# A fused decoder layer: the first transfers from one small tensor, through one queue, and 34 warm-up products instead of 40

## What is computed

```python
h = rms_norm(x, norm_w[l], NORM_EPS)          # x: 256 x 2048
proj = h @ w_in[l]                            # all float32
o_a = nsa_mixer(...)                          # its compression uses cmp_k_w1, cmp_v_w1 (4096 x 512 each)
o_b = diff_mixer(...)
mixed = jnp.concatenate([o_a * jax.nn.silu(z_a), o_b * jax.nn.silu(z_b)], axis=-1)
x = x + mixed @ w_out[l]
return rms_norm(x, final_norm_w, NORM_EPS)
```

## Time and profile before

| | |
|---|---|
| median of 3 runs | 494.6 us (493.87 to 495.35) |
| profiled execution, its time | 495.11 us |
| its span in the trace | 493.3 us |
| TensorE busy | 482.1 us (98%) |
| chain that ended last, share of TensorE | 96% |
| HBM read | 105.20 MB |

### The profile page before, as it was taken

How to read it: one execution, slowest core, us unless ns; L and a number is a source line. 1 busy time by engine, 2 the same in 40 slices (tenths; PEclk the granted TensorE clock), 3 DMA queues, 4 the chain that set the end, 5 groups by cost and what they waited for, 6 DMA issues and landing times.

```text
span 493.3 us, 6472 instructions
## 1 busy us (share of the span) xinstructions
PE 482.1 (98%) x2542; PEld 391.1 (79%) x2542; DVE 357.7 (73%) x496; ACT 222.0 (45%) x303; POOL 46.0 (9%) x51
## 2 busy tenths in 40 slices
PE   8999999999999999999999999999999999999993
PEld 7888867777777888888888888888888888888882
DVE  4765969368595897998798848488897998454542
ACT  5658423334333355445345454664535443434331
POOL 1003400020202002020020000002000000203051
PEclk9999999999999999999999999999999999999997
DMA  8999948778789434244253425435784454655005
GB/s 282 409 421 420 355 189 325 316 318 310 306 322 387 153 124 157 86 170 171 86 202 140 149 108 182 170 123 208 277 331 174 167 176 191 242 222 192 1 1 170
DMA packets 18013, 107.71 MB, mean 218 GB/s; under 512 B 2240, under 2 KB 2880, under 8 KB 6080
## 3 DMA queue, kind: packets, MB, share of 16 engines
q1 hardware_dynamic: 16112, 103.95, 55.3%
q10 hardware_dynamic: 1872, 3.36, 1.9%
HBM read 105.20 MB, written 2.10 MB: 218 GB/s over the span
## 4 chain that ended last, share of the span: by engine, by line
PE 96%; DMA 1%; DVE 1%; ACT 1%; issue 0%; POOL 0%; POOLq 0%; DVEq 0%; SPq 0%; ACTq 0%
PE acc L1083 26%; PE acc L1085 26%; PE acc L1084 26%; PE S L1228 3%; PE O L1122 3%; PE acc L1103 1%; PE acc L1106 1%; PE acc L1110 1%; PE S L1245 1%; DMA raw<-stream 1%; PE O L1269 1%; PE O L1263 1%; PE O L1264 1%; PE O L1265 1%; DVE wlo L708 0%; PE O L1148 0%
## 5 line engine op out<-in xcount | busy, mean ns | idle before, releaser
L708 DVE TENSOR_TENSOR wlo<-raw,whi 128x2048 fp32r<-128x2048 f32 x72 | 165.7, 2304 | 83.4 <-ACT whi L434 82.8
L434 ACT ACTIVATE whi<-raw 128x2048 fp32r<-128x2048 f32 x72 | 137.9, 1917 | 163.3 <-PE acc L1085 150.2
L1083 PE MATMUL acc<-whi,hT_hi 128*128 128x512 f32 x440 | 174.3, 396 | 0.0
L1084 PE MATMUL acc<-wlo,hT_hi 128*128 128x512 f32 x440 | 171.4, 390 | 0.0
L1085 PE MATMUL acc<-whi,hT_lo 128*128 128x512 f32 x440 | 171.4, 390 | 0.0
L1083 PEld LDWEIGHTS acc<-whi,hT_hi 128*128 128x128 f32 x440 | 82.6, 188 | 23.4 <-issue 6.7
L1085 PEld LDWEIGHTS acc<-whi,hT_lo 128*128 128x128 f32 x440 | 82.6, 188 | 17.5
L1084 PEld LDWEIGHTS acc<-wlo,hT_hi 128*128 128x128 f32 x440 | 82.7, 188 | 16.6
L381 POOL TENSOR_TENSOR stage<-stage,stage 128x512 f32<-128x512 f32 (+1 forms) x16 | 23.4, 1479 | 183.0 <-DVE stage L759 183.0
L516 ACT ACTIVATE e<-S,small 128x128 f32<-128x128 f32 (+1 forms) x48 | 19.6, 420 | 26.7 <-DVE small L805 26.7
L768 DVE STREAM_TRANSPOSE zT<-stage 32x256 f32<-32x256 f32 x64 | 27.9, 436 | 2.0
(11 more groups left out here) (172 smaller groups left out, 486.3 us busy)
## 6 DMA issues: line engine op xcount, KB each, us to landing
raw<-stream SPq DMA_DIRECT2D x72, 1024.0 KB, 4.9
row_raw<-stream SPq DMA_DIRECT2D x16, 1024.0 KB, 6.4
raw<-stream SPq DMA_DIRECT2D x6, 512.0 KB, 9.6
x_nat<-x_rows SPq DMA_DIRECT2D x2, 1024.0 KB, 15.5
x_nat<-x_rows SPq DMA_DIRECT2D x1, 2048.0 KB, 8.9
xTs<-xT SPq DMA_DIRECT2D x3, 512.0 KB, 12.6
result<-x_nat SPq DMA_DIRECT2D x6, 256.0 KB, 3.2
raw<-stream SPq DMA_DIRECT2D x4, 256.0 KB, 5.9
```

Of the source, the lines that this page charges most:

```text
L434: act.activation(whi[:, n % SPLIT, :], raw[:, n % RAW, :], ACT.Copy).then_inc(hi_ready, 1)
L708: dve.tensor_tensor(wlo[:, n % SPLIT, :], raw[:, n % RAW, :], whi[:, n % SPLIT, :].bitcast(f32), ALU.subtract)\
L1083: pe.matmul(acc_bank(n), xh, wh, start=k == 0, stop=False)
L1084: pe.matmul(acc_bank(n), xh, wl, start=False, stop=False)
```

## The change

SP now issues x pieces 1 and 2 itself, each right in front of the piece of chunk 0 that is used with it; ACT issues only `nw` before its table load. x and chunks 0 and 1 are laid into one tensor `head` of 128 rows of 32 KB (16 KB of x, then 8 KB of chunk 0, then 8 KB of chunk 1); `stream` begins with chunk 2. The warm-up is 34 products.

```diff
+HEAD_CHUNKS = 2
-WARM_UP = 40
+WARM_UP = 34
...
             k, n = X_PIECES[p]
-            eng.dma_start(xTs[:, k:k + n, :], xT[:, k:k + n, :]).then_inc(xT_in[p], 16)
+            at = head[:, k * SEQ:(k + n) * SEQ].rearrange("p (k s) -> p k s", k=n)
+            eng.dma_start(xTs[:, k:k + n, :], at).then_inc(xT_in[p], 16)
...
             for i, (c, k, n) in enumerate(W_PIECES):
-                if (c, k) in ((0, 0), (2, 0)):
-                    x_piece(sp, 0 if c == 0 else 3)
-                sp.dma_start(raw[:, c, k * NB:(k + n) * NB], stream[c, :, k * NB:(k + n) * NB]).then_inc(w_in[i], 16)
+                for p in (0, 1, 2, 3):
+                    if (c, k) == ((0, 0), (0, 1), (0, 2), (2, 0))[p]:
+                        x_piece(sp, p)
+                at = KT * SEQ + (CH * c + k) * NB
+                src = head[:, at:at + n * NB] if c < HEAD_CHUNKS else stream[c - HEAD_CHUNKS, :, k * NB:(k + n) * NB]
+                sp.dma_start(raw[:, c, k * NB:(k + n) * NB], src).then_inc(w_in[i], 16)
             x_piece(sp, 4)
             x_piece(sp, 5)
...
             act.dma_start(nw[:, :], norm_w).then_inc(nw_in, 16)
-            x_piece(act, 1)
-            x_piece(act, 2)
             act.wait_ge(warm_ready, 1)
...
-        "stream": a(np.stack([parts[k, b][j] for k, b, j in STREAM])),
+        "stream": a(np.stack([parts[k, b][j] for k, b, j in STREAM[HEAD_CHUNKS:]])),
         "w_gate": tiles(cols("gate")),
-        "xT": tiles(x.T),
+        "head": a(np.concatenate([tiles(x.T).reshape(P, -1)] + [parts[k, b][j] for k, b, j in STREAM[:HEAD_CHUNKS]], axis=1)),
```

More of the change, by code:

```diff
@@ L106, in unit_a, with program @@
     return u // 2, 1 + u % 2
-def program(nc, stream, w_gate, xT, x, norm_w, cmp_pos, ck_w2, cv_w2, lam, subln_w, final_w, consts, out):
+def program(nc, stream, w_gate, head, x, norm_w, cmp_pos, ck_w2, cv_w2, lam, subln_w, final_w, consts, out):
     f32, f32r, bf16 = mybir.dt.float32, mybir.dt.float32r, mybir.dt.bfloat16
@@ L324, in _ @@
                         wait_used(sp, ROWS[m - ROW_RAW])
-                    sp.dma_start(row_raw[:, m % ROW_RAW, :], stream[c, :, :]).then_inc(row_in[m % ROW_RAW], 16)
+                    sp.dma_start(row_raw[:, m % ROW_RAW, :], stream[c - HEAD_CHUNKS, :, :]).then_inc(row_in[m % ROW_RAW], 16)
                     continue
@@ L332, in _ @@
                     sp.dma_start(x_nat[:, :, :], x.rearrange("(t p) d -> p t d", p=P)).then_inc(x_in, 16)
-                sp.dma_start(raw[:, n % RAW, :], stream[c, :, :]).then_inc(raw_in[n % RAW], 16)
+                sp.dma_start(raw[:, n % RAW, :], stream[c - HEAD_CHUNKS, :, :]).then_inc(raw_in[n % RAW], 16)
                 if RAW < c <= RAW + TT:
```

## The result

The changed kernel takes 497.62 us (median of 10 runs, 495.61 to 499.13), the kernel before 494.81 us on the same chip (10 runs, 493.53 to 495.35): a ratio of 1.0065, 95% interval 1.005 to 1.008. It is slower by 0.65%, where 493.0 was forecast. The profiled execution took 497.82 us, its span is 496.0; before they were 495.11 and 493.3.

The account below looks back on a forecast made before the run. TensorE, busy 98% of the span, was taken as the bound, so only its start could gain. 1.15 + 0.6 = 1.75 us, under the 1.83 cut-off; 1.6 was taken from the median 494.6, giving 493.0 us, range 491.4 to 494.7.

Parts of the forecast that it names:

- The first product: At the start: the first weight piece lands at 4.9 instead of 6.05, so the first real product starts 1.15 us earlier.
- the slow stretch goes: Rival, at the start: reads run at some 400 GB/s from 2 us on; 2.7 us gained, 491.9 us; chance 0.18.
- The clock: First products at the start: lower clock costs 1.8 us; between -0.6 and all 1.8 back, the middle, 0.6 us, was taken.
- From the second tile on supply leads: Chunk 0 onward: TensorE takes 1.36 us a K tile, its 384 KB 0.95 us, so data stay ahead, narrowly up to chunk 1.
- the queue would cover the two more issues: SP's queue at the start: later pieces issued up to 1.2 us later, at no cost because issued transfers are already queued.
- a wait for later pieces in chunks 0 and 1: Sign, early chunks: if TensorE waits inside chunks 0 and 1 for later pieces, the prediction is wrong; no size given.
- The cut-off: At chunk 4, first split whole: gain limited to its 1.43 us margin plus 0.4 us from a faster stream, 1.83 us.
- Everything later runs back to back behind it, up to the last product: After the start: all later work follows the first real product without a break, so only its moment and the first pace matter.
- The 34 products themselves cost nothing as long as the data come at or after 4.85: Warm-up: 34 products end at 4.85 us, so the shorter warm-up costs 0 if data come no sooner.
- The slower one by the clock: Rival, at the start: data no sooner, TensorE idles 1.97 us, lower clock lasts longer; about 1.7 us lost, 496.3; chance 0.05.
- The one by the rows: Rival, reads of x and chunks 0 and 1: rows 32 KB apart read slower; at half rate 8.6 us lost, 503; chance 0.03.
- the one that the slow stretch belongs to the first microseconds: Rival, at the start: low rate stays, piece gains 0.3 to 0.6 us, 0.2 to 0.3 overall, 494.3 us; chance 0.29.

Follow-up runs that it names:

- e2: The kernel before with the warm-up cut from 40 to 34 products and nothing else: 499.23 us, ratio 1.0088.

## Why the prediction was wrong

**The first product**: predicted 1.15 us earlier (first `whi` at 4.9), measured 1.83 (4.21). The mechanism was the right one, though not the cause of most of it: of the `whi`'s time order and queue by themselves gain 0.42 us, the new tensor by itself 1.65. I had left the slow packets unexplained, and the rival "the slow stretch goes" put it down to two queues and three tensors; it was the reading from `stream`.

**The clock**: I took 0.6 us, the middle of -0.6 and 1.8. The higher level was there from the first product, so all of it came back. The reasoning by idle time doesn't hold, though. Ahead of the first product TensorE stood 0.5 us here and 2.0 in the kernel before with 34 products, and both were at the higher level at once; it stood 0.9 in the one with the order alone, 1.3 in the kernel before and 2.3 in the kernel before with 34 and 12 empty instructions, and these three had 0.85 a pair for three or four pairs. Its length alone doesn't order the cases.

**"From the second tile on supply leads"** was wrong. TensorE now caught up with the third piece of chunk 0, which came behind x tiles 2 and 3 in SP's queue, and waited 1.26 us; that the queue would cover the two more issues and the new order didn't hold for this piece. I had said that a wait for later pieces in chunks 0 and 1 would make the prediction wrong; of the 1.83 + 1.8 = 3.6 us of the first two terms it took 1.26. The forecast's sum stands in spite of it, because chunk 4 cut the lead to 1.47 anyway.

**The cut-off** 1.43 + 0.4 was right in kind: the new wait behind `wlo` is there (0.4 us), and the lead there is 1.47. Only the 0.4 was large; chunk 4 came 0.18 us sooner, because the stream was slower from 5 to 10 us.

**The step that failed** is in the first paragraph: "Everything later runs back to back behind it, up to the last product". It is the ground on which a lead at the start was carried over to the end, and it treats the warm-up's length as time only: "The 34 products themselves cost nothing as long as the data come at or after 4.85". They are also 12 instructions, and without them the code blocks end at other places in the work. One fetch then comes too late for a dense stretch: 2.23 us by the stop and 1.59 behind it, at the lower clock, 3.8 us in all, of which the lead pays 1.19. I hadn't looked at the instruction queues.

**The rivals.** The slower one by the clock gave 496.3, near to the measured time, but for another reason and at another place: the idle time at the start shrank, as the forecast said. The kernel before with 34 products met its condition, with 2.0 us of idle time, and was at the higher level all the same. The one by the rows is refuted by 368 to 382 GB/s at that pitch. So is the one that the slow stretch belongs to the first microseconds. The one that the slow stretch goes was nearest at the start, with 1.83 of its 1.97 us and all of the clock; but of the 1.3 us by which it let chunk 4 come sooner, 0.18 came.

**Even without the stop** the forecast was too good. With 12 empty instructions the ratio is 0.9989, some 0.5 us, not 1.6; its interval reaches 1.0001, and the medians, 494.14 and 494.15, show no gain at all. The two profiled executions differ by 1.4 (493.74 and 495.11), near the forecast; the medians don't bear it out. That the profiled execution of before was one of the slower ones is a part of it, and I had allowed 0.15 for that. As the level at the start follows no idle time that I can name, it may differ between executions of one kernel too; no run here shows that.

**What stays open.** The fetch takes 1.35 us, and in the changed kernel TensorE goes on only 1.26 us after its end; the traces show nothing in between. Why the fetch begins 1.2 us later when the list is 12 instructions shorter is argued, not shown: it fits that the point that asks for it, a fixed distance ahead in the list, has moved behind the waits in front of the 32 products. And e2's runs lie up to 500.67, higher than stop and clock of its trace explain; in its trace the last product is 3.1 us late, while the ratio makes it 4.4 and the medians 5.1.

## What to carry to other kernels

Take the number of instructions of an engine as a part of the change, even if they are warm-up or empty: look at the waits that end in "issue" and at the instruction queue wherever hundreds of short instructions follow each other, and try a shift of some instructions before you blame a transfer. Judge an edit by its parts: here the tensor was worth 0.24%, the order by itself nothing, the warm-up's number minus 0.8 to 0.9%, and only the sum was measured at first. Try a tensor of its own, read through both queues, for what the first microseconds need. Moving what isn't needed yet behind the chunk that is took a wait away, but wasn't shown to save time.

## What the runs showed of the hardware

- TensorE can stop at one place of its instruction list, which goes with a late code packet: 2.24 and 2.56 us, 0.46 and 0.22 with 4 and 8 instructions in front, none with 12, and 0.23 in the kernel before. It went on 1.2 to 1.5 us after the packet's end. That the place is a border of a code block is inferred from the packets' size and times.
- After that stop the granted clock was at half its level for 3.8 us (PEclk 0.52, products of 0.43 us), 1.6 us of time. In the kernel before with 34 products it was up for some products more and then low from 182.8 to 186.1. That the stop alone brings the fall wasn't tried by itself, but both kernels here with a stop of over 2 us had it, and none of the others.
- The column PEclk showed this fall, but 1.00 for products of the same 0.43 us at the start.
- With the first 256 KB pieces read from the 92 MB tensor the DMA engines moved 64 to 145 GB/s in each of the two microseconds between 3 and 5 us, in four kernels; from tensors of 2 or 4 MB 206 to 382, in nine. With the pieces of x on a second queue it was 316 to 382, with all on one 206 to 317. The reason is open: size, row pitch and place in memory changed together.
- From 5 to 8 us one queue gave 270 to 309 GB/s where two gave 331 to 422. The number of queues isn't shown to be the reason: the order differs as well, and the kernel with two small tensors, which has two queues, gave 287, 154 and 361.
